# Start of a decoder layer: full-row products of ones, GpSimd scaling three turned tiles, splits and loads in another order

## The reference

```python
h = rms_norm(x, ln1_g)
proj = h @ w_in                      # columns: h_q 384, h_kv 256, h_kr 32, q 512, kv 768, gates 24
q  = (rms_norm(h_q, cq_g) @ w_uq)    # group A: latent attention
kv = (rms_norm(h_kv, ckv_g) @ w_ukv)
mix = concat(rms_norm(mla(q, kv, h_kr)), rms_norm(nsa(...)))
x = x + mix @ w_o
x = x + square(relu(rms_norm(x, ln2_g) @ w_up)) @ w_down
```

## Time and profile before

| | us |
|---|---|
| median of 3 runs (lowest to highest) | 649.33 (648.38 to 651.1) |
| the profiled execution | 649.63 |
| its span, first to last instruction of the program | 647.8 |
| TensorE busy in the span | 637.1 |
| VectorE, ScalarE, GpSimd busy | 495.7, 403.2, 160.7 |

### The profile page before, as it was taken

One profiled execution on the slowest core, in us unless ns is written; L12 is line 12 of the kernel. 1 busy time (PEld: TensorE's weight loads), 2 busy tenths in 40 slices (PEclk: granted clock), 3 DMA queues, 4 the chain that ended last, 5 costly groups with the idle time before them and its releaser, 6 DMA issues.

```text
span 647.8 us, 11768 instructions
## 1 busy us (share of the span) xinstructions
PE 637.1 (98%) x4157; PEld 563.5 (87%) x4157; DVE 495.7 (77%) x931; ACT 403.2 (62%) x808; POOL 160.7 (25%) x230
## 2 busy tenths in 40 slices
PE   9999999999999999999999999999999999999998
PEld 5988888887779888887899999999998788888886
DVE  6275756479887888887885787778768999998675
ACT  7845667467897647566447666757657655655561
POOL 0426755443332201222110111111111221222200
PEclk9999999999999999999999999999999999999999
DMA  8583538998997964896371687878876898989983
GB/s 311 201 323 145 188 138 287 300 282 242 245 276 239 364 211 163 258 268 157 65 196 70 178 238 198 213 219 191 230 178 164 192 256 213 239 232 269 271 244 147
DMA packets 34650, 142.50 MB, mean 220 GB/s; under 512 B 5303, under 2 KB 5687, under 8 KB 33632
## 3 DMA queue, kind: packets, MB, share of 16 engines
q1 hardware_dynamic: 22688, 83.72, 36.6%
q0 software_dynamic: 10208, 34.88, 29.9%
q10 hardware_dynamic: 1696, 23.14, 9.4%
HBM read 139.57 MB, written 65.06 MB: 316 GB/s over the span
## 4 chain that ended last, share of the span: by engine, by line
PE 85%; ACT 3%; DVE 3%; issue 2%; DMA 1%; POOL 0%; ACTq 0%; DVEq 0%
PE bank L2080 14%; PE bank L2081 13%; PE bank L2082 13%; PE bank L2481 7%; PE bank L2483 7%; PE bank L2482 7%; PE bank L2100 6%; PE bank L2316 3%; PE bank L2259 2%; PE bank L2298 2%; PE bank L2413 2%; PE bank L2412 2%; PE bank L2411 2%; DMA raw<-weights 1%; PE bank L2270 1%
## 5 line engine op out<-in xcount | busy, mean ns | idle before, releaser
L849 POOL DMA_DIRECT2D down_sums<-w_down x64 | 49.9, 779 | 235.1 <-PE bank L2483 143.1
L1369 DVE TENSOR_TENSOR w_lo<-raw,w_hi 128x1024 fp32r<-128x1024 f32 (+3 forms) x70 | 79.9, 1154 | 24.8 <-ACT w_hi L947 24.3
L947 ACT ACTIVATE w_hi<-raw 128x1024 fp32r<-128x1024 f32 (+3 forms) x70 | 67.9, 991 | 39.9 <-DMA raw<-w_pairs 24.9
L2080 PE MATMUL bank<-w_hi,act_hi 128*128 128x512 f32 (+3 forms) x224 | 89.9, 401 | 1.9 <-DVE w_lo L1369 1.1
L2081 PE MATMUL bank<-w_lo,act_hi 128*128 128x512 f32 (+3 forms) x224 | 80.4, 359 | 0.0
L2082 PE MATMUL bank<-w_hi,act_lo 128*128 128x512 f32 (+3 forms) x224 | 80.3, 358 | 0.0
L1095 ACT ACTIVATE p_buf<-s_buf,stats 128x128 f32<-128x128 f32 (+3 forms) x96 | 53.8, 561 | 32.3 <-PE bank L2100 17.2
L1330 ACT ACTIVATE w_hi<-raw 128x1024 fp32r<-128x1024 f32 x31 | 32.8, 1059 | 36.8 <-DMA raw<-down_sums 18.8
L2080 PE MATMUL bank<-w_hi,s_all 128*128 128x512 f32 x140 | 54.6, 390 | 0.0
L2081 PE MATMUL bank<-w_lo,s_all 128*128 128x512 f32 x140 | 54.5, 389 | 0.0
L2082 PE MATMUL bank<-w_hi,s_all 128*128 128x512 f32 x140 | 54.5, 389 | 0.0
(11 more groups left out here) (313 smaller groups left out, 1829.2 us busy)
## 6 DMA issues: line engine op xcount, KB each, us to landing
down_sums<-w_down ACTq DMA_DIRECT2D x32, 512.0 KB, 6.2
down_sums<-w_down POOLq DMA_DIRECT2D x64, 256.0 KB, 5.7
raw<-down_sums SPq DMA_DIRECT2D x32, 512.0 KB, 5.6
up_sums<-w_pairs POOLq DMA_DIRECT2D x28, 512.0 KB, 10.0
raw<-up_sums SPq DMA_DIRECT2D x28, 512.0 KB, 4.7
raw<-weights SPq DMA_DIRECT2D x26, 512.0 KB, 5.9
up_sums<-w_pairs SPq DMA_DIRECT2D x16, 512.0 KB, 6.6
raw<-w_down SPq DMA_DIRECT2D x16, 512.0 KB, 5.4
```

The costliest lines, as they stand in the source:

```text
L849: pool.dma_start(sums_dram[k, rows_], a["w_down"][SUMS[m][1], step, rows_], accum_op=ALU.add, max_dma_last_dim=4096).then_inc(*sum_added[k ...
L947: ins = act.activation(hi[:, 0:width], raw[:, n % RAW, 0:width], ACT.Copy)
L1369: ins = dve.tensor_tensor(lo[:, 0:width], raw[:, n % RAW, 0:width], hi[:, 0:width].bitcast(F32), ALU.subtract)
L2080: pe.matmul(dst, a_h, w_h, start=start, stop=False, skip_group_check=onto)
```

## The change

Line numbers below are those of the kernel before; the same functions stand some 20 lines lower in the changed kernel.

1. The tile of ones has 128 rows in place of 1, and there are 3 products of ones in place of 5.
2. The gain and turned tile 0 are one array `x_first`, loaded by one transfer; the transfer of `gain1` on ScalarE's queue is gone. ScalarE begins with a copy of four numbers, before it waits for any data.
3. Turned tiles 1 to 3 are multiplied by the gain on GpSimd, in place, in halves of four feature blocks (128x512), ahead of all its other work. ScalarE then makes the high part of a half with one copy and VectorE the low part with one subtraction: 2 operations per tile and engine in place of 8. Tile 0 stays as it was, in two parts with the split of piece 0 between them.
4. GpSimd computes the roots of the cq sums ahead of the tables.
5. ScalarE and VectorE split pieces 5, 6 and 7 ahead of all four `cq_out` and `latent_row`; piece 2 is split ahead of tile 1, piece 3 between tiles 2 and 3.
6. TensorE takes pieces 0 to 2 tile by tile.
7. SP loads all four rows tiles `x` ahead of piece 4, `gain_c` at piece 4 and `consts` at piece 6.

```diff
-TURNED_AT, ROWS_AT = {0: (0,), 2: (1,), 3: (2, 3)}, {4: (0, 1), 5: (2,), 6: (3,)}
+TURNED_AT, ROWS_AT = {0: (0,), 2: (1,), 3: (2, 3)}, {4: (0, 1, 2, 3)}
-        warm = place("warm", 512, at=r_mla, parts=1)
+        warm = place("warm", 512, at=r_mla)
...
-                if n == 3:
+                if n == 4:
                     sp.dma_start(gain_c, a["gain_c"]).then_inc(*gainc_in.mark())
-                if n == 4:
+                if n == 6:
                     sp.dma_start(consts[:, P:CONST_LOADED], a["consts"][:, P:]).then_inc(*consts_in.mark())
...
             pool.wait_ge(*pool_step.at("half"))
+            pool.wait_ge(*xt_in[0].at())
+            for t in range(1, NT):
+                pool.wait_ge(*xt_in[t].at())
+                for half in range(2):
+                    rows_ = x_t[t][:, 4 * half:4 * half + 4, :]
+                    pool.tensor_tensor(rows_, rows_, gain1[:, 4 * half:4 * half + 4].unsqueeze(2).to_broadcast([P, 4, P]),
+                                       ALU.mult).then_inc(*pool_step.mark(("xg", t, half)))
...
+            for t in range(NT):
+                latent_rsqrt("cq", t)
 
             pool.wait_ge(*consts_in.at())
...
-            act.dma_start(gain1, a["gain_ln1"]).then_inc(*gain1_in.mark())
             act.dma_start(ident, a["consts"][:, 0:P]).then_inc(*ident_in.mark())
...
-            ln1_his(0)
+                for half in range(2):
+                    act.wait_ge(*pool_step.at(("xg", t, half)))
+                    act.activation(act_hi[:, 4 * half:4 * half + 4, t * P:(t + 1) * P], x_t[t][:, 4 * half:4 * half + 4, :],
+                                   ACT.Copy).then_inc(*turn_hi.mark(("ln1", t, half)))
+
+            act.wait_ge(*pool_step.at("half"))
+            act.activation(neg_rs, half_neg[:, 0:NT], ACT.Copy)
+            first_his(range(4))
             split_hi(SPLITS[0])
+            first_his(range(4, KD))
             split_hi(SPLITS[1])
+            split_hi(SPLITS[2])
             ln1_his(1)
-            split_hi(SPLITS[2])
             ln1_his(2)
+            split_hi(SPLITS[3])
             ln1_his(3)
-            split_hi(SPLITS[3])
             ln1_square(0)
...
-            cq_out(0)
-            cq_out(1)
-            cq_out(2)
             for m in (5, 6, 7):
                 split_hi(SPLITS[m])
-            cq_out(3)
+            for t in range(NT):
+                cq_out(t)
...
+                for half in range(2):
+                    ks, cols = slice(4 * half, 4 * half + 4), slice(t * P, (t + 1) * P)
+                    dve.wait_ge(*turn_hi.at(("ln1", t, half)))
+                    dve.tensor_tensor(act_lo[:, ks, cols], x_t[t][:, ks, :], act_hi[:, ks, cols].bitcast(F32),
+                                      ALU.subtract).then_inc(*turn_lo.mark(("ln1", t, half)))
...
+            for m in (5, 6, 7):
+                split_lo(SPLITS[m])
             dve.wait_ge(*gainc_in.at())
-            latent_row("cq", 0)
-            latent_row("cq", 1)
-            for m in (5, 6):
-                split_lo(SPLITS[m])
-            latent_row("cq", 2)
-            split_lo(SPLITS[7])
-            latent_row("cq", 3)
+            for t in range(NT):
+                latent_row("cq", t)
...
             pe.wait_ge(*dve_step.at("warm"))
-            for _ in range(5):
+            for _ in range(3):
                 pe.matmul(latent_bank(NT - 1), warm[:, 0:P], warm, start=True, stop=True)
-            latent_part("cq", 0, 0)
-            latent_part("cq", 1, 0)
-            latent_part("cq", 0, 1)
-            latent_part("cq", 1, 1)
-            for t in range(2):
-                latent_part("cq", 2, t)
-            for i in range(3):
-                latent_part("cq", i, 2)
-            for i in range(3):
-                latent_part("cq", i, 3)
+            for t in range(NT):
+                for i in range(3):
+                    latent_part("cq", i, t)
```

More of the change, by code:

```diff
@@ L392, in build @@
         c_lo = place("c_lo", 5 * SEQ, F32R, at=r_bias + 5 * SEQ * 4).rearrange("p (k s) -> p k s", k=5)
-        x_t = place("x_t", NT * D_MODEL, at=r_work).rearrange("p (t k s) -> p t k s", t=NT, k=KD)
+        x_later = place("x_t", (NT - 1) * D_MODEL, at=r_work).rearrange("p (t k s) -> p t k s", t=NT - 1, k=KD)
+        x_first = place("x_first", KD + D_MODEL, at=r_mk + 24576)
+        gain1 = x_first[:, 0:KD]
+        x_t = [x_first[:, KD:].rearrange("p (k s) -> p k s", k=KD)] + [x_later[:, t, :, :] for t in range(NT - 1)]
         ln_sq = place("ln_sq", D_MODEL + 1, at=r_mk + 16384)
@@ L532, in build @@
         pe_col, pe_lo, kc_ss, kc_rs = stat(2), stat(2), stat(1), stat(1)
-        gain1, neg_rs = stat(KD), stat(NT)
+        neg_rs = stat(NT)
         banks = [psum(f"bank{i}") for i in range(8)]
@@ L768, in _, with latent_rsqrt @@
             pool.dma_start(onehot, a["onehot"]).then_inc(*onehot_in.mark("table"))
+            def latent_rsqrt(b, t):
+                c, width = (t, Q_RANK) if b == "cq" else (NT + t, KV_RANK)
+                pool.wait_ge(*squares.at((b, t)))
+                rsqrt((b, t), rs_c[:, c:c + 1], ss_c[:, c:c + 1], width)
+            for t in range(NT):
+                latent_rsqrt("cq", t)
             pool.wait_ge(*consts_in.at())
@@ L784, in _ @@
                 ins.then_inc(*pool_step.mark(name))
-            for c, (b, width) in enumerate((("cq", Q_RANK), ("ckv", KV_RANK))):
-                for t in range(NT):
-                    pool.wait_ge(*squares.at((b, t)))
-                    rsqrt((b, t), rs_c[:, c * NT + t:c * NT + t + 1], ss_c[:, c * NT + t:c * NT + t + 1], width)
+            for t in range(NT):
+                latent_rsqrt("ckv", t)
             for t in range(NT):
@@ L1383, in to_lo, with first_lows @@
                 dve.tensor_tensor(dst, src, hi.bitcast(F32), ALU.subtract).then_inc(*turn_lo.mark(key))
-            def ln1_lows(t):
-                for k in range(KD):
-                    if k % 2 == 0:
-                        dve.wait_ge(*turn_hi.at(("ln1", t, k // 2)))
-                    cols = slice(t * P, (t + 1) * P)
-                    ins = dve.scalar_tensor_tensor(act_lo[:, k, cols], x_t[:, t, k, :], gain1[:, k:k + 1],
-                                                   act_hi[:, k, cols].bitcast(F32), ALU.mult, ALU.subtract)
-                    if k % 2:
-                        ins.then_inc(*turn_lo.mark(("ln1", t, k // 2)))
+            def first_lows(ks):
+                for k in ks:
+                    if k % 2 == 0:
+                        dve.wait_ge(*turn_hi.at(("ln1", 0, k // 2)))
+                    ins = dve.scalar_tensor_tensor(act_lo[:, k, 0:P], x_t[0][:, k, :], gain1[:, k:k + 1],
+                                                   act_hi[:, k, 0:P].bitcast(F32), ALU.mult, ALU.subtract)
+                    if k % 2:
+                        ins.then_inc(*turn_lo.mark(("ln1", 0, k // 2)))
+            def ln1_lows(t):
+                for half in range(2):
[3 more added lines that the diff above has]
+                                      ALU.subtract).then_inc(*turn_lo.mark(("ln1", t, half)))
             def ln2_rows(t, cols=slice(0, D_MODEL)):
@@ L1411, in _ @@
             dve.memset(warm, 1.0).then_inc(*dve_step.mark("warm"))
-            dve.wait_ge(*gain1_in.at())
-            ln1_lows(0)
+            first_lows(range(4))
             split_lo(SPLITS[0])
+            first_lows(range(4, KD))
             split_lo(SPLITS[1])
+            split_lo(SPLITS[2])
             ln1_lows(1)
-            split_lo(SPLITS[2])
             ln1_lows(2)
+            split_lo(SPLITS[3])
             ln1_lows(3)
-            split_lo(SPLITS[3])
             split_lo(SPLITS[4])
```

27 lines of the change are left out of this document (15 added, 12 removed).

## The result

The changed kernel takes 646.10 us, median of six executions (644.98 to 646.79), against 649.37 for the kernel before (648.38 to 651.19): ratio 0.9942 on record, 95% interval 0.9923 to 0.9962 (the quotient of the two medians is 0.9950). Between the medians that is 3.3 us less, where 1.9 us less was forecast. The profiled execution took 645.1 us with a span of 643.3, so 4.5 us less than its counterpart before. Most of this difference between 4.5 and 3.3 turns out to have a cause of its own.

The account below looks back on a forecast made before the run. TensorE, busy 637.1 of 647.8 us, was taken as the bound, so gains before 60 us should arrive nearly whole. 1.3 us (wait at 33.80) plus 0.6 (wait at 52.94) gave 1.9 off 649.33: 647.4 us, range 643.6 to 649.6.

Parts of the forecast that it names:

- Case A: In the cq stage GpSimd's multiplies and VectorE take turns; gain 1.9 us, time 645.8 to 648.7; chance 0.52.
- case C: TensorE's clock isn't held up early; up to 1.6 us of the gain goes, 649.0 us; chance 0.14.
- B: The multiplies don't disturb VectorE; sixth ends at 15.9, gain 5.1 us, 644.2 us; chance 0.28.
- Start: ScalarE's table load moves ahead of the data; first copy about 4.55, TensorE starts at 7.85 not 10.26, 2.4 us earlier.
- The turns: GpSimd's six multiplies, each blocking VectorE 1.10 us, alternate with its splits; sixth ends at 19.2, cq sums at 28.5 to 28.6.
- cq_out behind them: ScalarE waits for GpSimd; first cq_out ends at 28.45, fourth at 32.5, and the ckv parts follow them.
- Loads: SP's queue: piece 4 lands near 20 (wanted 22.3), piece 7 near 25.3 (wanted 26.8), hidden by ScalarE's squares.
- The wait at 33.80: TensorE's 0.89 us wait for piece 5's low part goes; ckv's second round starts at 32.5, gaining 1.3 us.
- The wait at 52.94: TensorE's 0.59 us wait for ScalarE goes, as loads are issued some 7 us earlier; gain 0.6 us.
- recorded signs: Multiplies 1.9 to 2.2 us beside VectorE, splits of pieces 1 and 2 near 2, TensorE idling 4 to 6 us.
- the sign for B: GpSimd's six 128x512 multiply rows ending before 17 us would show that they don't disturb VectorE.
- D: Slower: a multiply above 1.58 us eats the gain; at 2.1 us the kernel takes 652.4 us; chance 0.06.

Follow-up runs that it names:

- a_one_late: Changed kernel with one-row products of ones and ScalarE's table load back behind the first tile's arrival (added copy removed); 645.58 us.
- a_extra: Changed kernel with two further 128x512 multiplies on GpSimd, on turned tile 0 into scratch, product unused; 648.65 us.
- b_new_roots: Kernel before with one edit, GpSimd making the four cq roots ahead of the rotary tables; 648.68 us, ratio 0.9980.
- a_old_both: Changed kernel with the splits of pieces 5 to 7 back in their old places and the cq roots back behind the tables; 647.76 us.
- a_old_splits: Changed kernel with the splits of pieces 5 to 7 back behind the third cq_out on ScalarE and between latent rows on VectorE; 647.06 us.
- a_old_roots: Changed kernel with only GpSimd's cq roots back behind the tables; 646.08 us.
- b_full_row: Kernel before with its products of ones on all 128 rows and nothing else changed; 650.76 us, ratio 1.0020.
- a_no_mult: Changed kernel with GpSimd's multiplies undone, tiles 1 to 3 made by eight operations each on ScalarE and VectorE as before; 645.62 us.
- a_fill: Changed kernel with TensorE's waits before 12.2 us filled by further full-row products of ones; 645.13 us.
- a_one_row: Changed kernel with its three products of ones on one row instead of 128; 645.27 us.
- a_one_no: Changed kernel with one-row products of ones and without the multiplies on GpSimd; 645.20 us.

## Why the prediction came out as it did

The forecast was 647.4 us with a range of 643.6 to 649.6; 646.10 is inside it. Case A is the one that came, with one term mis-sized, and a share of C.

That the number is so near has some luck in it. With the multiply at its measured size, case A's own rule gives a gain of 3.3 to 3.5 us, and the medians show 3.3. But the profiled execution, whose clock doesn't fall, gained 4.5, nearer to B's 5.1, and the fall in other executions took about 1 us of it back. The 2.6 us above the forecast's 1.9 are 2.06 at the second round of ckv (30.44 for 32.5), 0.26 at the wait of 52.94 (0.86 for 0.6), and 0.2 behind 640 us.

**Start.** Right. First copy at 4.46 (4.55 forecast), the low part of piece 0 done at 7.46 (7.7), first product at 7.61 (7.85). The forecast ascribed the early table load to its move ahead of the data, by the added copy; a_one_late has it as early without that copy.

**The turns.** Right in kind, wrong in size: this is the step that failed. "Of a multiply I count 1.10 as blocking (1.26 less the part before it needs the data)" rested on two rows of other widths. Measured beside small operations only, it is 1.04 us (a_extra), 0.24 less than recorded. Six times 0.24 is 1.4 us; the sixth ended at 17.34 in place of 19.2 (the first also began 0.24 us sooner), and the ckv sums start at 27.25 in place of 28.5 to 28.6. Case A named this: with 1.00 the gain grows by 1.6 to 3.5 us. Several of the recorded signs failed by the same step. The rows beside VectorE last 1.5 to 1.75 us and not 1.9 to 2.2; the split of piece 1 isn't stretched (0.95), since it came just ahead of the first multiply, and only that of piece 2 is (1.75); TensorE waits for 2.0 us between 8 and 18 us and not for 4 to 6; and the sixth row ends so near to 17, the sign for B, that only the stretched rows tell A from B.

**cq_out behind them.** Mostly the same error, carried on: the last half tile is copied by 18.0 and not by 19.9, which is 1.9 of the 2.2 us by which `cq_out` starts sooner. Forecast: the first `cq_out` ends at 28.45, the fourth at 32.5, and TensorE follows them. Measured: the first starts at 25.19 (so ends near 26.2), the fourth ended by 29.4, and no part of ckv waits. The second round stands at 30.44 rather than 32.5: 1.3 us from the sums, 0.8 from this.

**Loads.** Right in the main. Forecast: piece 7 lands near 25.3, wanted at 26.8. ScalarE was ready for it earlier and waited 0.29 us, to 24.60; no wait of TensorE came of it.

**The wait at 33.80.** It went, as forecast, but its cause was told by half. "A wait of 0.89 us ending at 33.80, for the low part of piece 5, which stands on VectorE behind two `latent_row`": true, and the row ahead of it shows these rows themselves waiting 9.30 us for GpSimd. The first round of ckv took 5.08 us before. With the roots moved alone in that kernel it takes 4.03 (b_new_roots). Around the changed kernel it takes 4.32 with neither (a_old_both), 4.01 with the roots alone (a_old_splits) and 3.19 with the splits alone (a_old_roots). So moving the splits takes the waits away by itself, moving the roots takes away half of the excess in the kernel before and about a quarter in the changed one, and with the splits moved the roots add nothing (646.08 against 646.10). In medians the two edits together are worth 647.76 - 646.10 = 1.7 us. The rest, from before to a_old_both, is 649.83 - 647.76 = 2.1 us. Neither the multiplies nor the full-row ones add to it. By subtraction that leaves the start, the loads, TensorE's order tile by tile and the places of the splits of pieces 2 and 3; no run takes these apart. (The two make 3.8 us, which is what the ratio of 0.9942 gives, against 3.3 between the medians.)

**The wait at 52.94.** Gone, 0.6 us, as forecast. It is back, at 1.16 us, in a_old_both and not in a_old_splits nor a_old_roots, and gone in b_new_roots: either of the two edits removes it. In b_full_row, where TensorE runs 1.0 us later by then, it is gone without them.

**The clock, case C.** It got 0.14, and it happened in part. Of the six executions of the changed kernel two have a clock of 1.00 and took 644.98 and 645.10 us; four have 0.995 to 0.997 and took 645.95 to 646.79. The profiled one is of the first kind. a_old_roots parts likewise: 645.12, 645.53 and 645.76 at 1.00, 646.39, 646.46 and 646.48 at 0.997. Where the fall is seen (a_old_splits, a_no_mult, a_old_roots, a_extra) it comes between 10 and 13 us, behind the waits for low parts, and nine to sixteen products are slow. That this is also what the four executions of the changed kernel had is inferred, since no trace of one was taken; a_fill, which keeps TensorE busy there, and a_one_row, whose slow products lie under the waits, have 1.00 ten times out of ten and 644.98 to 645.61 us. It explains most of the difference between the 4.5 us of the profiled executions and the 3.3 of the medians: 1.0 us is the changed kernel's profiled execution under its median, 0.3 the other kernel's over its own. Not every execution obeys: a_no_mult took 644.77 us at 0.997 and a_one_late 647.88 at 1.00.

**B and D.** Both fall. VectorE was disturbed (1.75 for 0.96 us), and a multiply costs 1.04 us, far under the 1.58 that would have eaten the gain.

**What each edit is worth**, by these runs: the order of splits and roots 1.7 us; the other edits of order and loading, the early start among them, about 2 us together, by subtraction; the multiplies nothing that the medians show; the full-row ones nothing, or up to 0.8 us of harm where the clock falls (645.27 without them against 646.10; the two intervals overlap). The simplest good version is a_one_no at 645.20 us: the changed kernel without its multiplies and with one-row ones.

## What to carry to other kernels

When an engine waits for a low part, read one row further back, to what the instruction ahead of it waited for; here these rows had waited 9.30 us for a root that a third engine made only behind its tables, and moving the splits would have done without moving the roots. Moving elementwise work to GpSimd beside a busy VectorE bought nothing here, where the two took turns, though it saved instructions: count turns, and take the size of an unseen operation as a range that the sum is run through. And an early gain that only makes a later wait longer can be lost whole, because TensorE's clock can be down behind that wait (b_full_row). Two ways to keep it gave a steady clock here: filling such waits (a_fill) and letting the slow products lie under them (a_one_row).

## What had not been expected of the hardware

- Raising TensorE's clock sooner didn't make a kernel faster and by the medians made it slower: b_full_row, 650.76 against 649.63 us. Its trace has 1.52 us of work in 4 us and eleven slow products behind them; it doesn't show the whole loss.
- 8.9 us of products of ones on one row left the products behind them 0.32 us apart; with 128 rows, the only difference in b_full_row, they stood 0.17 us apart from the first group on.
- Idle stretches of 1 to 2 us with little work between cost the clock in some executions and not in others of one kernel (the changed one: 4 of 6, by their clock of 0.995 to 0.997; with a wait of 2.19 us in a_extra: 10 of 10).
- The granted clock reads 1.00 in the first 12 us of the kernel before, though the products stand 0.32 us apart there as they do at 0.50 in a_old_splits; the low level at the start of a kernel is seen in the spacing alone. Windows of the kernel before:

```profile
12.00:14.00 2.00, 2.00 (x8) 2.00 (x8) 2.00 (x7) 2.00 (x7) 0.00 (x0) 1.00 0.96 339
```

- GpSimd's multiply of 128x512 with one factor repeated over 128 columns takes 1.04 us, less than the 1.30 that its rows of 128 and 256 columns (0.46 and 0.74) let expect.
- The table load stood behind a wait for data (4.64 us) where the first copy waited for two transfers, and ahead of it (1.18 us, a_one_late) where it waited for one; that the number decides it isn't shown.
